# Rotary score products of an attention head loop padded from 64 to 128 rows

## What is computed

```
s = (jnp.einsum('bqhr,bkr->bhqk', qs, ckv)
     + jnp.einsum('bqhe,bke->bhqk', qr, krope)).astype(jnp.float32) * MLA_SCALE
s = jnp.where(key_pos[None, :] <= qpos[:, None], s, -jnp.inf)
p = jax.nn.softmax(s, axis=-1).astype(ckv.dtype)
```

## Time and profile before

| | |
|---|---|
| median of 3 runs | 1460.79 us |
| the runs | 1461.09, 1460.79, 1452.14 us |
| the profiled execution | 1451.67 us, its span 1450.0 us |
| mean granted clock of TensorE | 0.965 of 2.4 GHz |
| PE busy | 1364.2 us, 94% of the span |
| PE weight loads | 1257.6 us, 87% |
| DVE, ACT busy | 606.3 us (42%), 410.7 us (28%) |
| chain that ended last | PE 78%, SP's queue 7%, DVE 7%, ACT 3% |
| lines on that chain | L2104 24%, L2132 22% (MLP), L1350 6%, L1656 2%, L1665 1% |

### The profile page before, as it was taken

One profiled execution on the slowest core, in us unless ns is written; L12 is line 12 of the kernel. 1 busy time (PEld: TensorE's weight loads), 2 busy tenths in 40 slices (PEclk: granted clock), 3 DMA queues, 4 the chain that ended last, 5 costly groups with the idle time before them and its releaser, 6 DMA issues.

```text
span 1450.0 us, 22137 instructions
## 1 busy us (share of the span) xinstructions
PE 1364.2 (94%) x8796; PEld 1257.6 (87%) x8796; DVE 606.3 (42%) x949; ACT 410.7 (28%) x676; POOL 158.7 (11%) x195
## 2 busy tenths in 40 slices
PE   7998999999688998799999999999999999999996
PEld 7976777887566666699999999999999999999996
DVE  4122221545856565566542322423224232242558
ACT  4222232226433333534530311203113031130225
POOL 4433342010000000023100000000000000004022
PEclk9999999999889997899999999999999999999998
DMA  8668887232200002141130210202102021020103
GB/s 289 195 209 259 275 280 225 77 94 83 88 19 1 9 1 87 29 132 30 32 115 1 82 36 29 87 0 77 39 29 87 0 73 43 29 87 0 58 1 117
DMA packets 100593, 123.38 MB, mean 85 GB/s; under 512 B 11123, under 2 KB 84997, under 8 KB 100518
## 3 DMA queue, kind: packets, MB, share of 16 engines
q1 hardware_dynamic: 94374, 105.59, 23.0%
q0 software_dynamic: 6144, 16.79, 3.8%
HBM read 108.42 MB, written 13.93 MB: 84 GB/s over the span
## 4 chain that ended last, share of the span: by engine, by line
PE 78%; SPq 7%; DVE 7%; ACT 3%; issue 3%; DMA 2%; POOL 0%; DVEq 0%; ACTq 0%; POOLq 0%
PE psum L2104 24%; PE psum L2132 22%; PE psum L355 8%; PE psum L1827 6%; PE psum L1350 6%; SPq L267 3%; SPq L270 3%; PE psum L2071 3%; PE psum L1656 2%; PE psum L2065 2%; PE psum L1665 1%; DVE pT_lo L1737 1%; ACT p_rows L1696 1%; PE psum L904 1%; DVE softmax_stats L1719 1%
## 5 line engine op out<-in xcount | busy, mean ns | idle before, releaser
L2161 ACT ACTIVATE hid_tmp<-psum 128x1032 f32<-128x1032 f32 x32 | 33.1, 1034 | 531.2 <-PE psum L2104 526.5
L355 PE MATMUL psum<-xTh,win_hi 128*128 128x344 f32 (+1 forms) x432 | 149.4, 346 | 9.9 <-DVE xTl L408 9.9
L2104 PE MATMUL psum<-x_hi,w_hi 128*128 128x344 f32 x720 | 153.3, 321 | 0.0
L2104 PE MATMUL psum<-x_lo,w_hi 128*128 128x344 f32 x720 | 152.8, 321 | 0.0
L2104 PE MATMUL psum<-x_hi,w_lo 128*128 128x344 f32 x720 | 152.1, 320 | 0.0
L2132 PE MATMUL psum<-hid_hi,w_hi 128*128 128x344 f32 x672 | 142.5, 320 | 0.0
L2132 PE MATMUL psum<-hid_lo,w_hi 128*128 128x344 f32 x672 | 142.4, 320 | 0.0
L2132 PE MATMUL psum<-hid_hi,w_lo 128*128 128x344 f32 x672 | 141.8, 319 | 0.0
L355 PE MATMUL psum<-xTh,win_lo 128*128 128x344 f32 (+1 forms) x432 | 140.7, 326 | 0.0
L355 PE MATMUL psum<-xTl,win_hi 128*128 128x344 f32 (+1 forms) x432 | 140.6, 325 | 0.0
L2226 DVE TENSOR_TENSOR z_T<-z_T,psum 128x1032 f32<-128x1032 f32 x48 | 59.0, 1229 | 186.5 <-PE psum L2132 186.5
(11 more groups left out here) (379 smaller groups left out, 2197.5 us busy)
## 6 DMA issues: line engine op xcount, KB each, us to landing
mlp_raw<-in_w SPq DMA_DIRECT2D x64, 512.0 KB, 4.2
k_pages<-in_pages SPq DMA_DIRECT2D x128, 160.0 KB, 3.0
v_pages<-in_pages POOLq DMA_DIRECT2D x128, 128.0 KB, 4.4
win_raw<-in_w_in SPq DMA_DIRECT2D x17, 512.0 KB, 6.9
scratch<-proj_stage SPq DMA_DIRECT2D x13, 516.0 KB, 5.6
x_T_raw<-in_x_T SPq DMA_DIRECT2D x6, 688.0 KB, 9.3
z_T<-in_x_T SPq DMA_DIRECT2D x3, 1376.0 KB, 6.2
out_y_T<-z_T SPq DMA_DIRECT2D x12, 344.0 KB, 2.4
```

Source lines behind the costliest of these rows:

```text
L355: mm = pe.matmul(psum[0:M, 3 * (m % 2) + b, 0:BLK], w[:, m % 2, k, 0:M], x[:, k, b * BLK:(b + 1) * BLK], start=(k == 0 and i == 0), stop=( ...
L2104: mm = pe.matmul(psum[:, 3 * (i % 2) + b, 0:BLK], w[:, i % 2, k], x[:, k, C3[b]], start=(k == 0 and n == 0), stop=(k == KD - 1 and n == 2))
L2161: act.activation(ht[:, i % 2, :].rearrange("p (b c) -> p b c", b=3), mlp_set(i), ACT.Relu).then_inc(h_free, 1)
```

## The change

The key's rotary part is kept in two versions. The even one (`krope_even_*`) is multiplied with a constant column that is 1 in partitions 0 to 63 and 0 below; the odd one (`krope_odd_*`) with the opposite column. A head uses the version of its own parity with all 128 rows of the query tile, so that the other head's query rows meet zeros. The odd version lies in `mixT` rows 0 and 2. So heads 1 and 3 run first, which write rows 1 and 3, and heads 0 and 2 last; what lay in `mixT` rows 0 and 1 goes to 1 and 3, and the states go to 0 and 2. The odd version is written after the states have been stored, and so ACT and DVE wait for `gst_stored` in the setup. The constant columns take the place of three unused ones.

```diff
-        kz = [mixT[0:NB, r, 0:TP].rearrange("p (b c) -> p b c", b=4) for r in range(2)]
-        state = [mixT[:, 2 + r, 0:TP].rearrange("p (b f v) -> p b f v", b=4, f=2) for r in range(2)]
+        kz = [mixT[0:NB, 1 + 2 * r, 0:TP].rearrange("p (b c) -> p b c", b=4) for r in range(2)]
+        state = [mixT[:, 2 * r, 0:TP].rearrange("p (b f v) -> p b f v", b=4, f=2) for r in range(2)]
...
-        krh, krl = (sb(at + i * TP, f"krope_{n}", [P, TP], F32R) for i, n in enumerate(("hi", "lo"))); at += 2 * TP
+        kre = [sb(at + i * TP, f"krope_even_{n}", [P, TP], F32R) for i, n in enumerate(("hi", "lo"))]; at += 2 * TP
+        kro = [sb(PERSIST + 2 * i * T, f"krope_odd_{n}", [P, TP], F32R) for i, n in enumerate(("hi", "lo"))]
+        krh, krl = (kre[0], kro[0]), (kre[1], kro[1])
...
-        cksq = [mixT[:, r, 0:TP] for r in range(2)]
-        rope = [mixT[:, r, 0:TP] for r in range(2)]
+        cksq = [mixT[:, 1 + 2 * r, 0:TP] for r in range(2)]
+        rope = [mixT[:, 1 + 2 * r, 0:TP] for r in range(2)]
...
-            if name == "kr":
-                return krh[:], krl[:], krd[:], None
+            if name[:2] == "kr":
+                i = int(name[2])
+                return krh[i][:], krl[i][:], krd[:], const("half")[:, i:i + 1]
...
+        HEAD = (1, 3, 0, 2)
...
-            hi_of(act, "kr")
+            hi_of(act, "kr0")
+            act.wait_ge(gst_stored, 80)
+            hi_of(act, "kr1")
...
-            lo_of(dve, "kr"), lo_of(dve, "uv")
+            lo_of(dve, "kr0")
+            dve.wait_ge(gst_stored, 80)
+            lo_of(dve, "kr1"), lo_of(dve, "uv")
...
-                qc, r = slice(i * P, (i + 1) * P), slice(ROPE * (h % 2), ROPE * (h % 2) + ROPE)
+                qc, pr, odd = slice(i * P, (i + 1) * P), HEAD[h] // 2, HEAD[h] % 2
...
-                                                 ((qrh[r, h // 2, qc], qrl[r, h // 2, qc]), (krh[r, kc], krl[r, kc]))])
+                                                 ((qrh[:, pr, qc], qrl[:, pr, qc]), (krh[odd][:, kc], krl[odd][:, kc]))])
...
-        K_ORDER = [4, 5, 6, 7, 0, 1, 2, 3]
+        K_ORDER = [4, 5, 6, 7, *HEAD]
```

More of the change, by code:

```diff
@@ L64 @@
 for _n, _w in (("ident", P), ("ones", P), ("swap", P), ("tri16", P), ("chunkmask", P), ("causal", P),
-               ("dup", P), ("swapdup", P), ("pad", 272), ("sel4", 4), ("rowmask", 4)):
+               ("dup", P), ("swapdup", P), ("pad", 272), ("sel4", 4), ("rowmask", 1), ("half", 2), ("end", 1)):
     CONST_COLS[_n] = (_at, _w)
@@ L1299, in hymba_step @@
         C2 = [slice(b * 512, b * 512 + 512) for b in range(2)]
-        SPLITS = ["wr", "cq0", "cq1", "cq2", "ck0", "ck1", "kr", "uv", "q0", "q1"] + [f"v{t}" for t in range(8)]
+        SPLITS = ["wr", "cq0", "cq1", "cq2", "ck0", "ck1", "kr0", "kr1", "uv", "q0", "q1"] + [f"v{t}" for t in range(8)]
         def split_parts(name):
@@ L1402, in load_head @@
             uq = a["w_uq"].rearrange("l (k p) (h c) -> p (l k) h c", p=P, h=HEADS)
-            sp.dma_start(wqraw[:, 0:3, :], uq[:, :, h, 0:NOPE]).then_inc(wh_loaded, 16)
-            sp.dma_start(wqraw[:, 3:5, :], a["w_uk"].rearrange("l (k p) h n -> p (l k) h n", p=P)[:, :, h, :]).then_inc(wh_loaded, 16)
+            sp.dma_start(wqraw[:, 0:3, :], uq[:, :, HEAD[h], 0:NOPE]).then_inc(wh_loaded, 16)
+            sp.dma_start(wqraw[:, 3:5, :], a["w_uk"].rearrange("l (k p) h n -> p (l k) h n", p=P)[:, :, HEAD[h], :]).then_inc(wh_loaded, 16)
         def pe_norm_sums(pe, o, squares):
@@ L1633, in scores @@
                     if h == 0:
-                        split(pe, "kr")
+                        split(pe, "kr1")
                         mb.read(pe, ("v", 7)), mb.read(pe, ("v", 6))
@@ L1655, in values @@
                     for n, (vv, pp) in enumerate(((vh, pth), (vh, ptl), (vl, pth))):
-                        mm = pe.matmul(wk.of(key)[:, q0:512], vv[:, j, h * P:(h + 1) * P], pp[:, j, q0:512],
+                        mm = pe.matmul(wk.of(key)[:, q0:512], vv[:, j, HEAD[h] * P:(HEAD[h] + 1) * P], pp[:, j, q0:512],
                                        start=(j == 0 and n == 0), stop=(j == 4 * hf + 3 and n == 2))
@@ L1731, in dve_mla @@
                     wk.wait(dve, key)
-                    wk.free(dve.tensor_copy(mixT[:, h, hf * 512:hf * 512 + 512], wk.of(key)), key)
+                    wk.free(dve.tensor_copy(mixT[:, HEAD[h], hf * 512:hf * 512 + 512], wk.of(key)), key)
                 u = v - 2
@@ L1871, in act_out @@
             for i, k in enumerate(K_ORDER):
-                if k == 0:
+                if i == 4:
                     wk.read(act, ("pv", HEADS - 1, 1)), wk.read(act, ("pv", HEADS - 1, 0))
@@ L2454, in _tables @@
     put("sel4", (i % 32 < 16) & (i % 4 == h))
-    put("rowmask", np.where((i % 32) // 4 == i // 32, 0.0, -30000.0) + 0.0 * h)
+    put("rowmask", np.where((i % 32) // 4 == i // 32, 0.0, -30000.0))
+    put("half", i // ROPE == np.arange(2)[None, :])
     inv = 10000.0 ** (-np.arange(0, ROPE, 2, dtype=np.float64) / ROPE)
```

## The result

The changed kernel took 1447.0 us (median of 10 executions, 1443.45 to 1450.35), the kernel before 1456.75 (1452.14 to 1461.09, 10 executions). The ratio is 0.994, 95% interval 0.9922 to 0.9958: some 9 us faster (9.7 between the medians, 6 to 11 by the interval). The profiled execution took 1443.45 us, span 1441.8, mean granted clock 0.971.

A forecast was written before the change was run, and what follows sets the result against it. PE was taken to bound the head loop mostly, not always. 1451.7 - 9.0 (switches) - 3.0 (clock) + 1.3 (setup) = 1441; with most of the 9 us between executions taken away, 1443 us, 80% range 1435 to 1456.

The forecast's parts named there:

- The price of a switch: Score products on PE: each change between 64 and 128 rows costs 0.19 us at 2.4 GHz, 0.30 at 1.2.
- Switches on the chain: Head loop: removed switches on PE's chain save 9.5 us over four heads, taken as 9.0 after DVE and ACT's ring.
- The clock term in the fourth head: Clock returns to 2.4 GHz during the first scores after 565 us, saving 3.0 us (bounds 0 and 5).
- the signs set beforehand: Profile after: even score starts, no load gaps, second head about 40 us, fourth 53, no 13.5 us half-clock stretch with PE busy.
- What is late next: Head loop: DVE and ACT's ring per unit takes 0.1 us of the second head's switch gain, similar in each head.
- The rival of the ring: Head loop: half the switch gain becomes PE's waiting and the clock does nothing, 1448.5 us or 1457; chance 0.12.
- Setup, +1.3 us: Attention setup: DVE makes one more 128x1024 key low part, 1.28 us, all of it showing.
- new waits: Setup: ACT's and DVE's waits for the GLA stores cost nothing, with 16 us of cover.
- From the profiled execution to the median: Whole kernel: most of the 9 us between executions taken away, so 1443 on the sum's 1441; 1450 if they stay.
- The slower rivals: Score products or loop: padded weight loads exposed (1462 or 1471 us, chance 0.02), or more half clock (1470, 0.05).
- the one with more half clock: PV and query products: PE idles longer, clock stays at 1.2 GHz, costing 20 us against 11 gained: 1470; chance 0.05.
- The padded weight loads: Rotary score products: 144 loads exposed at 0.19 us, 18 us on the chain, 1462 or 1471 us; chance 0.02.

The follow-up runs named there:

- the two alternating kernels: A piece's six score products alternate non-rotary and rotary: in the kernel before (64 rows) 1512.9 us, in the changed kernel (128 rows) 1445.7 us.
- two profiles with 64 rows: The kernel before (ratio 1) and the changed kernel with rotary score products back at the head's 64 rows (ratio 1.0016).
- four with 128: Changed kernel (0.994), its repeat (0.9947), with products alternating (0.9938), and with both constant columns at 1 so the key isn't zeroed (0.9952).
- the rows undone: Changed kernel with rotary score products taking only the head's 64 rows again, layout and head order kept: 1457.6 us, ratio 1.0016 to the kernel before.
- the two kernels with moved low parts: Changed kernel with the key's low parts in DVE's setup waits: 1443.6 us; the same with ACT's high-part copy before the exponential: 1428.0 us.

## Why the prediction was right, and where its sizes were off

- **The price of a switch.** Right, 0.19 and 0.30, by the distances after the change and by the two alternating kernels.
- **Switches on the chain, 9.0 us, and the clock, 3.0.** The loop fell by 10.8 us in the profiled pair, and by 10.5 between the means of two profiles with 64 rows (177.1) and four with 128 (166.6), against 12.0. The term of the switches was right where it can be seen alone: with the rows undone the first head ran without half clock and took 33.45 us, in the changed kernel 30.94, so 2.5 less, where the sum has 2.65. In the second head it was 4.1: the PV products of the earlier trace rows's head, x24 partly at half clock, went from 6.86 to 4.89 us, 2.0, a clock gain that the sum didn't have; the other 2.1 answer to the 2.3 of the sum.
- **The clock term in the fourth head.** The mechanism held: with 128 rows a stretch at half clock that begins among the scores of that head lasted from 559.9 to 563.3, 3.4 us, and ended among scores; with the rows undone one lasted from 566.1 to 579.7, 13.6 us, as that of the earlier trace rows did, with PE as busy. (That of the earlier trace rows ended at 579.4, within the PV products of 576.77 and not behind them.) The windows of the two stretches, first of the changed kernel, then of the one with the rows undone:

```profile
560.00:563.20 3.20, 3.20 (x12) 3.10 (x11) 2.26 (x6) 1.87 (x4) 0.00 (x0) 0.50 0.04 15
```

```profile
566.20:579.60 13.40, 13.40 (x34) 9.00 (x34) 8.79 (x19) 5.12 (x10) 0.00 (x0) 0.50 0.17 56
```

  But its place was wrong. The 3.0 us, and the 2.1 of switches beside them, did not come in the fourth head, which got 0.9 us longer in this pair and 0.2 shorter on the means. Its chain from 556 to 570 us is now all DVE and ACT, the ring plus the preparation of the output weights between units:

```profile
562.31 0.38 ACT pT_hi L1710
562.69 1.05 ACT wout_sum_out L1867 x2
...
563.76 1.16 ACT wout_split L1868
...
564.95 1.29 DVE wout_split L1873
```

  PE idles there, and the clock fell elsewhere in the head (542.8 to 549.6, 570.1 to 573.5), so that PV products ran slower: the x12 takes 3.69 us against 3.27, and the x24 before it 6.65 against 4.88. The chain's rows of the x24, before and after:

```profile
553.74 4.88 PE psum L1656 x24
```

```profile
545.82 6.65 PE psum L1664 x24
```

  The half clock on the x24 is this execution's; in the other three profiles with 128 rows it takes 4.86 to 4.88 us. In exchange heads 1 to 3 lost their half-clock stretches (17.0 us in the profile before), which the sum had left in place. By heads: the first three gained 11.7 us where the sum has 7.25 for their switches, the fourth lost 0.9 where it has 5.3 to gain. The two errors nearly cancel, so that the total came out right is partly luck. Of the signs set beforehand, 40 us for the second head came out at 38.3, and 53 for the fourth at 57.7 to 60.0.
- **What is late next.** In the second head the 0.1 us was right: from the x15 to the PV x12 the chain took 15.60 us before (476.27 to 491.87) and 14.19 after (474.28 to 488.47), 1.4 less, where the switches of the x15, the first x12 and the x21 come to 1.5. The sum also implied the waiting: PE's busy time in the loop fell by 23.0 us (153.2 to 130.2), 12.0 of that were to show, and 10.8 did; the rest became PE's waiting for DVE and ACT. What failed is the fourth head: the sum gave the ring some 0.1 us of its switches and 0.6 of its clock term (3.6 cut to 3.0), and the ring, with the output weights' preparation in it, took nearly all. The rival of the ring holds for that head alone.
- **Setup, +1.3 us.** By the table, leaving out the two kernels with moved low parts: 44.3 us on the mean of the four without the second key part, 45.3 of the eight with it. So +1.0. At equal half clock in the setup it is +1.1 (43.4 against 44.5 and 44.6 at 13.7 us) and +0.9 (44.6 against 45.5 on the means at 17.1 us): right, a little high. The **new waits** cost nothing, right.
- **From the profiled execution to the median.** The forecast of 1443 lies 4 us below 1447. The execution profiled after took 1443.45, against a sum of 1441. The 9 us between executions were read as a kind that the change would mostly take away; 29 executions of the kernel before spread over 1446 to 1464 us, and the ten of the changed one still over 7. That term of the forecast was too large, and its start too: the median of 1460.79 was of three executions, that of ten is 1456.75. From 1460.79 to 1443 it forecast a fall of 17.8 us; 9.7 came. The median lies 5.1 us above the profiled execution before (1456.75 and 1451.67) and 3.6 after, where the forecast puts 2 on the sum.
- The slower rivals didn't come. (The 1470 of the one with more half clock counts from the median of 1460.79; from the profiled execution, as the other sums do, it would be 1461.) The padded weight loads hide as the 128-row ones did: the load of 492.86 runs under the product of 492.63. The rule of the Trainium skill ("TensorE: Matmul & The Clock Gate", Part 3) would have exposed them, and the trace of after disagrees with it as the earlier trace rows did.

## What to carry to other kernels

Read the starts of products and not their durations: a group with fewer rows amid full ones costs two switches, whatever its size, and padding with zeros was cheaper than the switches here, because the padded operand was made once (1.3 us of DVE) and used in 48 pieces. When an engine's work is cut by a few us in many places, walk the other engines' ring before booking the gain: here one exchange of two ACT instructions was worth more than the change itself, 14 us against 9. Whether it would have been worth as much in the kernel before was not run; the ring stood on that chain too. A term for the clock can be right in kind and land in another place.

## What the runs showed of the hardware that I had not expected

- The clock stayed at 1.2 GHz for 13.5 us in which PE's records show no pause, with changes of rows among the score products, and in the alternating kernel with 64 rows again from 462 to 475.5 with PE busy 13.50 of 13.50 us. Without switches the stretch in the same place ended after 3.4 us. A record of PE as fully busy doesn't tell which clock it has.
- One 64-row product between 128-row ones costs as much as three, 0.385 us at 2.4 GHz for the two switches, and the lower clock goes with it (0.963 against 0.967 to 0.969).
- The mean granted clock over the executions was 0.961 to 0.962 with the kernel before and 0.967 to 0.968 with the changed one: of 1450 us, 2 x 0.006 x 1450 = 17 us less at half clock (an estimate; each us at half clock takes half a us off the mean). The loops show as much, 41.0 and 47.8 us against 23.9 to 27.3. At half clock 17 us do the work of 8.7, so that is the most it can have brought, of a gain of 9 that also holds the switches; part of it fell where PE waits.
